# Output rows' norms: row sums inside VectorE's passes, squares on ScalarE, no wide GpSimd passes; the router's logits on four column strips of TensorE

## The chip, the cores and the metric

The kernel runs on one core of one Trainium2 chip. The metric is the device time of one execution in microseconds (us). A profile records one execution of the core: what each engine did and when (TensorE is PE, its weight loads PEld; VectorE is DVE, ScalarE is ACT, GpSimd is POOL, SyncE is SP), what it waited for, and the clock that TensorE was granted.

## The reference, cut to what matters

One layer of a streaming encoder on 1024 prompt rows and 64 sample rows of width 1024: a mixer, and then a mixture of 16 experts. The part that the change touches lies between the two, for every row:

```
mixed = w_out projection of the mixer's output
x   = LN_m(alpha * x + gate_m(c) * mixed)             # called x1 in the kernel; gains g, b
h   = LN0(x) * (1 + scale_f(c)) + shift_f(c)          # called h2
g_logits = h @ w_group + b_group                      # 4 columns
e_logits = h @ w_router + b_router                    # 16 columns
# group by argmax, two experts of the group by top_k, their weights by softmax
y   = sum over the two experts of weight * w_down(silu(h w_gate) * (h w_up))
x   = LN_f(alpha * x + gate_f(c) * y)
```

LN is a mean and a variance over the 1024 columns of a row, and LN0 is LN without gains.

## The kernel before, in words

Rows go in 9 tiles of up to 128, in the order `ORDER` = 0, 1, 2, 3, 8, 4, 5, 6, 7 (tile 8 has the 64 sample rows). Each engine has a program of its own, written in order; they meet at semaphores. Products of the projections and experts are split into three (high and low parts of both operands), so 48 matmuls of 512 columns make one tile's output projection.

The stage in question is a loop over those 9 tiles; n is a tile's place in `ORDER`, and `END` = 8 is the last place.

- TensorE (`out_part`, `h2_turned`, `logits`): for tile n the 48 matmuls of the projection into one of two pairs of banks; then `logits(n - 3)`, then `h2_turned(n - 2)`, eight transpositions of h2. After the last tile follow three rounds for the tiles still open, with `keep_clock` between them: matmuls of constants that fill the waits. `logits` multiplies the turned rows (weights of 128 columns) with `router_w` (20 columns moving), eight chunks, each as two instructions.
- VectorE: reads the projection (L1866), adds alpha x (L1868), takes mean and variance (`bn_stats`, L1616), subtracts the mean and applies the gain (L1881), makes the low part of tile n + 2's operand (`out_low`, L1791 and L1793), finishes x1 (L1888) and takes mean and variance of x1. The last tile is read in two halves (L1875 to L1877), and its h2 is made on VectorE too (L1897, L1900).
- GpSimd: the power -0.5 of each variance (`first_power` L2113, `norm_scalars` L639 to L641), and for the first eight tiles two passes of 1024 columns over h2, the scale (L2123) and the shift (L2125).
- ScalarE: the high part of tile n + 2's operand, the copy of the turned rows out of PSUM (L1500), and h2's normalisation (L1508).
- SP's queue: the loads of x, the stores of x1 and h2, and, behind the last of them, the weights of expert 0 (L773).

Behind the loop the router's decisions are made on VectorE (from L1905, which reads the logits), lists of rows are built, the first rows are gathered by a DMA, and a loop runs over 26 blocks of expert rows. The final norms, in the kernel's last stage, already use the two forms that the change takes up here: a pass on VectorE that also sums its result along the row (`accum_out`, L2032), and a `Square` on ScalarE with the negated mean as its bias, which sums the squares (L1585).

## Time and profile before

| what | before |
|---|---|
| median of 3 runs | 1382.14 us (1380.56 to 1382.39) |
| the profiled execution | 1381.44 us |
| its span, first to last instruction | 1379.6 us |
| TensorE busy over the span | 1307.4 us, 95% |
| VectorE, ScalarE, GpSimd busy | 768.3, 544.1, 318.0 us |

The profile is of an execution of its own; times in it count from the first instruction, and 1.84 us of the execution lie outside the span. Busy times of the whole span say little here: the stage of the change lasts from 675 to some 809 us, and it has limits of its own.

### The profile page before, as it was taken

To read this page: it belongs to the slowest core of one execution; us is meant where nothing else is said; L and a number is where in the kernel's file an instruction comes from. 1 tells how busy PE (TensorE), PEld (TensorE's weight loads), DVE (VectorE), ACT (ScalarE), POOL (GpSimd) and SP (SyncE) were. 2 spreads that over 40 slices of the span, in tenths; PEclk is the share of its full clock that TensorE was granted. 3 is DMA by queue.
4 is the path that set the end of the run, shared out by engine and by line. 5 is a ranking of instruction groups with operands and counts; after the bars stand their busy time and mean duration, and the time that the engine had idled before them with its cause. 6 is when DMAs were issued, how large, how long until landed. Compare 5 with 4: busy or idle time off the path is not lost.

```text
span 1379.6 us, 20025 instructions
## 1 busy us (share of the span) xinstructions
PE 1307.4 (95%) x7293; PEld 1015.5 (74%) x7294; DVE 768.3 (56%) x1040; ACT 544.1 (39%) x750; POOL 318.0 (23%) x449
## 2 busy tenths in 40 slices
PE   4899999999999989999999989999999999999984
PEld 2666678898787756666687877888888888888851
DVE  5734232424502066666699974557888242559648
ACT  0432012332212156556512242457776232357522
POOL 0123320002200066667256521000000000000053
PEclk9999999999999999999999999999999999999997
DMA  9853320102121171211432368867999261649764
GB/s 332 321 183 125 124 69 1 62 1 77 42 66 35 49 215 32 62 32 33 153 108 92 115 244 327 328 236 279 398 399 398 86 240 61 243 158 398 288 222 166
DMA packets 138776, 234.54 MB, mean 170 GB/s; under 512 B 57328, under 2 KB 58936, under 8 KB 138712
## 3 DMA queue, kind: packets, MB, share of 16 engines
q1 hardware_dynamic: 128440, 196.41, 40.3%
q0 software_dynamic: 6496, 23.60, 4.9%
q10 hardware_dynamic: 3776, 13.67, 2.4%
q8 instruction: 42, 0.69, 0.2%
q14 instruction: 22, 0.18, 0.0%
HBM read 197.96 MB, written 35.68 MB: 169 GB/s over the span
## 4 chain that ended last, share of the span: by engine, by line
PE 77%; POOL 7%; DVE 6%; issue 5%; DMA 2%; ACT 1%; SPq 1%; POOLq 0%; ACTq 0%; DVEq 0%
PE psum L834 71%; POOL arena L2101 5%; DMA arena<-in_w_ada_mix 2%; PE psum L1246 2%; PE psum L1061 1%; PE psum L1252 1%; DVE arena L2040 1%; DVE arena L2039 1%; PE psum L941 1%; DVE arena L2032 1%; DVE arena L2031 1%; PE psum L885 1%; PE psum L1155 0%; POOL arena L2098 0%; SPq L656 0%
## 5 line engine op out<-in xcount | busy, mean ns | idle before, releaser
L834 PE MATMUL psum<-arena 128*64 128x128 f32 (+8 forms) x1396 | 168.6, 374 | 25.5 <-DMA arena<-in_w_ada_mix 16.7
L834 PE MATMUL psum<-win_high,x_low 128*128 128x512 f32 (+1 forms) x432 | 168.7, 391 | 0.0
L834 PE MATMUL psum<-win_high,x_high 128*128 128x512 f32 (+1 forms) x416 | 166.3, 400 | 0.0
L834 PE MATMUL psum<-high,h_high 128*128 128x512 f32 x416 | 162.1, 390 | 2.5 <-DVE h_low L1986 2.5
L834 PE MATMUL psum<-win_low,x_high 128*128 128x512 f32 (+1 forms) x416 | 162.5, 391 | 0.0
L834 PE MATMUL psum<-high,h_low 128*128 128x512 f32 x416 | 162.2, 390 | 0.0
L834 PEld LDWEIGHTS psum<-arena 128*64 128x64 f32 (+4 forms) x1396 | 83.8, 144 | 103.5 <-issue 72.7
L1981 DVE TENSOR_TENSOR low_odd<-raw_odd,high 128x2048 fp32r<-128x2048 f32 x48 | 108.0, 2287 | 37.2 <-ACT high L1522 37.1
L1981 DVE TENSOR_TENSOR low_even<-raw_even,high 128x2048 fp32r<-128x2048 f32 x48 | 107.9, 2287 | 37.0 <-ACT high L1522 36.5
L1842 DVE TENSOR_TENSOR_SCAN arena<-arena,psum 128x512 f32<-128x512 f32 (+3 forms) x112 | 108.2, 1004 | 19.7 <-ACT arena L1477 19.5
L2101 POOL TENSOR_TENSOR arena<-arena 128x512 f32<-128x512 f32 (+4 forms) x116 | 96.8, 835 | 9.5 <-POOL arena L2095 0.3
L834 PEld LDWEIGHTS psum<-win_high,x_high 128*128 128x128 f32 (+1 forms) x416 | 75.6, 182 | 30.3 <-issue 8.7
L2158 POOL COPY smalls<-smalls 128x1 int32 x26 | 4.7, 181 | 404.4 <-PE psum L1246 398.9
L834 PEld LDWEIGHTS psum<-win_high,x_low 128*128 128x128 f32 (+1 forms) x432 | 78.6, 182 | 20.0
L1522 ACT ACTIVATE high<-raw_even 128x2048 fp32r<-128x2048 f32 x48 | 89.3, 1909 | 8.1 <-ACT arena L1563 5.3
L834 PEld LDWEIGHTS psum<-high,h_high 128*128 128x128 f32 x416 | 78.1, 188 | 18.9 <-issue 2.8
L1522 ACT ACTIVATE high<-raw_odd 128x2048 fp32r<-128x2048 f32 x48 | 89.3, 1912 | 6.4 <-ACT arena L1563 6.1
L834 PEld LDWEIGHTS psum<-high,h_low 128*128 128x128 f32 x416 | 78.1, 188 | 16.2
L834 PEld LDWEIGHTS psum<-win_low,x_high 128*128 128x128 f32 (+1 forms) x416 | 75.7, 182 | 17.3
L834 PE MATMUL psum<-high,a_high 128*128 128x512 f32 x208 | 83.3, 400 | 2.4
L834 PE MATMUL psum<-low_even,h_high 128*128 128x512 f32 x208 | 81.0, 390 | 0.0
L834 PE MATMUL psum<-low_odd,h_high 128*128 128x512 f32 x208 | 81.0, 389 | 0.0
(258 smaller groups left out, 2381.1 us busy)
## 6 DMA issues: line engine op xcount, KB each, us to landing
raw_even<-in_w_e_gate SPq DMA_DIRECT2D x8, 2048.0 KB, 10.9
raw_even<-in_w_e_up SPq DMA_DIRECT2D x8, 2048.0 KB, 16.8
raw_even<-in_w_e_down SPq DMA_DIRECT2D x8, 2048.0 KB, 15.6
raw_odd<-in_w_e_gate SPq DMA_DIRECT2D x8, 2048.0 KB, 10.6
raw_odd<-in_w_e_up SPq DMA_DIRECT2D x8, 2048.0 KB, 17.0
raw_odd<-in_w_e_down SPq DMA_DIRECT2D x8, 2048.0 KB, 16.0
win<-in_w_in SPq DMA_DIRECT2D x7, 2048.0 KB, 8.4
expert_rows<-arena ACTq DMA_DIRECT2D x26, 512.0 KB, 6.3
```

Source lines behind the costliest of these rows:

```text
L834: pe_last[0] = nc.tensor.matmul(*x, **y)
L885: last = nc.tensor.transpose(bank(H_BANKS[n % 4])[:, c0:c0 + r], xt[0:r, t, k * P:(k + 1) * P], ident[0:r, 0:r])
L941: last = nc.tensor.transpose(b[:, h * P:h * P + r], src[0:r, h, :], ident[0:r, 0:r])
L1061: last = nc.tensor.transpose(turned_weights(s)[0:r, a_, j * P:(j + 1) * P], weight[:, s % 3, a_, j * P:j * P + r], ident)
L1246: last = nc.tensor.transpose(psum[1][:, c // 4, (c % 4) * P:(c % 4 + 1) * P], hg[:, c * P:(c + 1) * P], ident)
L1252: last = nc.tensor.transpose(bank(at)[:, (f - f0) * P:(f - f0 + 1) * P], an[:, f * P:(f + 1) * P], ident)
L1522: A(chunk(high_w, c), chunk(raw_w[k], c), ACT.Copy).then_inc(s_wH, 1)
L1842: V.tensor_tensor_scan(out, out, floor, init, ALU.mult, ALU.max).then_inc(s_scan, 1)
L1981: TT(chunk(low_w[k], c), chunk(raw_w[k], c), chunk(high_w, c).bitcast(F32), ALU.subtract).then_inc(s_wL, 1)
L2031: done(TT(x, psum[2 * (t % 2)][0:r].rearrange("p a c -> p (a c)"), rows8[0:r, int(t == LAST)], ALU.mult), s_gated, t + 1)
L2032: done(STT(x, x1c[t][0:r], ALPHA, x, ALU.mult, ALU.add, accum_out=fin_nm[0:r, t:t + 1]), s_cacc, t + 1)
L2101: G.tensor_tensor(weight[:, s % 3, a_, 0:w], p[:, lo + 1:513], p[:, lo:512], ALU.subtract).then_inc(s_wm, 1)
```

## The change

Six things are changed, all in that stage.

1. VectorE's pass that adds alpha x also sums its result (`accum_out` into `ln_nmr`); a small operation makes the negated mean of it. The same is done for x1. `bn_stats` is gone for all tiles but the last.
2. ScalarE squares the rows less their mean and sums them (`accum_out` into `ln_ve`), twice a tile: once for x1's norm, once for h2's. It no longer normalises h2.
3. GpSimd keeps only operations of one column: scale and epsilon, and the power, twice a tile.
4. VectorE makes h2 of every tile in two passes; the second one (`h2_finished`) stands in the next tile's sequence.
5. The logits: `logit_parts(n)` keeps `router_w` (now padded to 32 columns) as the weights and moves the turned rows; chunk k goes to the strip of 32 PSUM partitions k % 4, two chunks added on each strip. ScalarE copies the 128 partitions out (`lparts`), and `logits(n)`, one matmul with a constant `pick`, adds the four strips and turns the result back. `logits` is one tile further behind than `logit_parts`.
6. The loads of the router's weights move in SP's queue from the projections' stage to behind the first two loads of x, since `router_w` now lies where the attention's queries were; the constant `pick` is loaded in their old place.

```diff
             def logits(n):
                 t = ORDER[n]
                 r = rows_of(t)
-                pe.wait_ge(s_hte, n + 1)
-                if n == 0:
-                    pe.wait_ge(s_router, 64)
-                for k in range(KC):
-                    last = mm(bank(6)[0:r, t * 20:t * 20 + 20], h2T[:, k, 0:r], router_w[:, k, :],
-                              start=(k == 0), stop=(k == KC - 1))
-                last.then_inc(s_lg, 1)
+                pe.wait_ge(s_hte, 2 * n + 2)
+                mm(bank(6)[0:r, t * 20:t * 20 + 20], lparts[:, 0:r], pick, start=True, stop=True).then_inc(s_lg, 1)
...
+            def logit_parts(n):
+
+                r = rows_of(ORDER[n])
+                pe.wait_ge(s_hte, 2 * n + 1)
+                if n == 0:
+                    pe.wait_ge(s_router, 80)
+                for k in range(KC):
+                    j = 32 * (k % 4)
+                    last = mm(bank(6)[j:j + 32, 256:256 + r], router_w[:, k, :], h2T[:, k, 0:r],
+                              start=(k < 4), stop=(k >= 4))
+                last.then_inc(s_lp, 1)
...
+                if n >= 4:
+                    logits(n - 4)
                 if n >= 3:
-                    logits(n - 3)
+                    logit_parts(n - 3)
                 if n >= 2:
                     h2_turned(n - 2)
...
+            def logit_parts(n):
+
+                r = rows_of(ORDER[n])
+                act.wait_ge(s_lp, n + 1)
+                A(lparts[:, 0:r], bank(6)[:, 256:256 + r], ACT.Copy).then_inc(s_hte, 1)
+
             for n in range(TILES + 2):
                 if n + 2 < TILES:
                     out_high("mixed", ORDER[n + 2])
+                if n < END:
...
+                    act.wait_ge(s_ve1, n + 1)
+                    A(xin[0:r, n % 2], t1[0:r, n % 2], ACT.Square, bias=ln_nmr[0:r, t:t + 1],
+                      accum_out=ln_ve[0:r, t:t + 1]).then_inc(s_sq5, 1)
                 v = n - 2
                 if v >= 0:
                     r = rows_of(ORDER[v])
                     act.wait_ge(s_ht, v + 1)
                     if v:
-                        act.wait_ge(s_lg, v)
+                        logit_parts(v - 1)
                     A(h2T[:, :, 0:r], psum[2].rearrange("p a (c q) -> p (a c) q", q=P)[:, :, 0:r], ACT.Copy).then_inc(s_hte, 1)
                 if n < END:
...
-                    act.wait_ge(s_nm2, n + 1)
...
-                    A(h2[0:r, n % 2], x1[0:r, n % 2], ACT.Identity, bias=ln_nmr[0:r, 9 + t:10 + t],
-                      scale=ln_rstd[0:r, 9 + t:10 + t]).then_inc(s_h2a, 1)
+                    act.wait_ge(s_ve2, n + 1)
+                    A(t1[0:r, n % 2], x1[0:r, n % 2], ACT.Square, bias=ln_nmr[0:r, 9 + t:10 + t],
+                      accum_out=ln_ve[0:r, 9 + t:10 + t]).then_inc(s_sq5, 1)
+            logit_parts(END)
...
+            def h2_finished(n):
...
+                dve.wait_ge(s_nm2, n + 1)
+                done(STT(h, h, ln_rstd[0:r, 9 + t:10 + t], rows5[0:r, 4 + int(t == LAST)], ALU.mult, ALU.add), s_h2, n + 1)
+
+            for n, t in enumerate(ORDER[:END]):
...
+                if n >= 2:
+                    dve.wait_ge(s_sq5, 2 * (n - 2) + 2)
+                dve.wait_ge(s_op, n + 1)
+                done(TT(x, psum[n % 2][0:r].rearrange("p a b -> p (a b)"), rows5[0:r, s], ALU.mult), s_ope, n + 1)
+                dve.wait_ge(s_x5[n % 2], 16 * (n // 2 + 1))
+                step(STT(x, xin[0:r, n % 2], ALPHA, x, ALU.mult, ALU.add, accum_out=ln_nmr[0:r, c]))
+                mean_negated(r, c, s_ve1, n + 1)
...
+                step(STT(y, x, ln_nmr[0:r, c], rows5[0:r, 6], ALU.add, ALU.mult))
+                if n >= 1:
+                    h2_finished(n - 1)
                 if n + 2 < TILES:
                     out_low("mixed", ORDER[n + 2])
                 dve.wait_ge(s_nm1, n + 1)
...
+                done(STT(y, y, ln_rstd[0:r, c], rows5[0:r, 7], ALU.mult, ALU.add, accum_out=ln_nmr[0:r, c2]), s_x1, n + 1)
+                mean_negated(r, c2, s_ve2, n + 1)
...
+                step(STT(h, y, ln_nmr[0:r, c2], rows5[0:r, 2 + s], ALU.add, ALU.mult))
+            h2_finished(END - 1)
...
             for n, t in enumerate(ORDER[:END]):
                 r = rows_of(t)
...
-                norm_scalars(step, G, r, 9 + t).then_inc(s_nm2, 1)
-                pool.wait_ge(s_h2a, n + 1)
-                step(G.tensor_tensor(h, h, rows5[0:r, 2 + s], ALU.mult))
-                first_power(n + 1)
-                G.tensor_tensor(h, h, rows5[0:r, 4 + s], ALU.add).then_inc(s_h2, 1)
...
+                for i, (col, ready) in enumerate(((t, s_nm1), (9 + t, s_nm2))):
+                    pool.wait_ge(s_sq5, 2 * n + i + 1)
+                    step(G.tensor_scalar(ln_ve[0:r, col:col + 1], ln_ve[0:r, col:col + 1], 1.0 / D, EPS, ALU.mult, ALU.add))
+                    power(col, r).then_inc(ready, 1)
...
             load_x(0)
             load_x(1)
+            sp.dma_start(router_w[:, :, 0:4], w_group[0].rearrange("(k p) n -> p k n", p=P)).then_inc(s_router, 16)
+            sp.dma_start(router_w[:, :, 4:20], w_router[0].rearrange("(k p) n -> p k n", p=P)).then_inc(s_router, 16)
```

The pieces stand in the order of the engines' programs: TensorE, ScalarE, VectorE, GpSimd, SP. In SP's loop the loads of x wait for ScalarE's first square of a tile instead of VectorE's variance. The last tile keeps its program on VectorE; its rows are now read by nothing on GpSimd but the two powers.

On VectorE, one tile in the middle of the loop (n = 6) stood so before (the numbers at L lines are those of each version's own text):

```order
L1866 TENSOR_TENSOR arena<-psum,arena 128x1024
L1868 SCALAR_TENSOR_TENSOR arena<-arena 128x1024
L1616 BN_STATS smalls<-arena 128x6 x2
L1617 BN_AGGR smalls<-smalls 128x2
L1856 TENSOR_SCALAR smalls<-smalls 128x1
L1881 SCALAR_TENSOR_TENSOR arena<-arena,smalls 128x1024
L1791 TENSOR_TENSOR x_low<-mixed,mix_high 128x4x128
L1793 TENSOR_TENSOR x_low<-hT,mix_high 128x4x128
L1888 SCALAR_TENSOR_TENSOR arena<-arena,smalls 128x1024
L1616 BN_STATS smalls<-arena 128x6 x2
L1617 BN_AGGR smalls<-smalls 128x2
L1856 TENSOR_SCALAR smalls<-smalls 128x1
```

And so stands the tile n = 7 and the step behind it in the changed kernel, the last tile of the new loop:

```order
L1906 TENSOR_TENSOR arena<-psum,arena 128x1024
L1908 SCALAR_TENSOR_TENSOR arena,smalls<-arena 128x1024
L1888 TENSOR_SCALAR smalls<-smalls 128x1
L1914 SCALAR_TENSOR_TENSOR arena<-arena,smalls 128x1024
L1896 SCALAR_TENSOR_TENSOR arena<-arena,smalls 128x1024
L1920 SCALAR_TENSOR_TENSOR arena,smalls<-arena,smalls 128x1024
L1888 TENSOR_SCALAR smalls<-smalls 128x1
L1927 SCALAR_TENSOR_TENSOR arena<-arena,smalls 128x1024
L1896 SCALAR_TENSOR_TENSOR arena<-arena,smalls 128x1024
L1937 TENSOR_TENSOR arena<-psum,arena 128x512
```

The two passes over the rows for mean and variance are gone, and two passes for h2 have come (L1927 and L1896); L1896 is `h2_finished`, first for the tile before, then, behind the loop, for this one, ahead of the last tile's first half (L1937).

On TensorE, the end of the stage stood so before, from the last projection's last matmul on (128x20 are the logits, L1155 the transpositions, 128x256 the fillers):

```order
L834 MATMUL psum<-x_high,x_low 128x512
L834 MATMUL psum<-smalls,arena 128x20 x8
L1155 MATMUL psum<-smalls,arena 128x128 x8
L834 MATMUL psum<-smalls 128x256 x2
L834 MATMUL psum<-smalls,arena 128x20 x8
L834 MATMUL psum<-smalls 128x256 x3
L1155 MATMUL psum<-smalls,arena 128x128 x8
L834 MATMUL psum<-smalls 128x256 x2
L834 MATMUL psum<-smalls,arena 128x20 x8
L834 MATMUL psum<-smalls 128x256 x6
L1155 MATMUL psum<-smalls,arena 128x128 x8
```

And so in the changed kernel:

```order
L841 MATMUL psum<-smalls 64x20
L841 MATMUL psum<-arena 32x128 x8
L1162 MATMUL psum<-smalls,arena 128x128 x8
L841 MATMUL psum<-smalls 128x256 x2
L841 MATMUL psum<-smalls 128x20
L841 MATMUL psum<-arena 32x128 x8
L841 MATMUL psum<-smalls 128x256 x3
L1162 MATMUL psum<-smalls,arena 128x128 x8
L841 MATMUL psum<-smalls 128x20
L841 MATMUL psum<-smalls 128x256 x2
L841 MATMUL psum<-arena 32x128 x8
L841 MATMUL psum<-smalls 128x256 x6
```

Each group of eight 128x20 products has become eight products of 32x128 and, one tile later, a single 128x20; the fillers are the same, with one more ahead of the very last single product.

## Rows read from the trace of the kernel before

**Rows 1.** Stage of the output rows: busy us of PE, PEld, DVE, ACT, POOL; clock.

```profile
675.00:788.00 113.00, 112.57 (x566) 91.79 (x567) 104.35 (x131) 27.43 (x41) 55.22 (x47) 1.00 0.36 123
```

**Rows 2.** Chain of waits that ended last, 640 to 860: start, us, what.

```profile
750.90 10.93 PE psum L834 x48
...
761.92 1.24 DVE arena L1866
...
837.90 11.17 PE psum L834 x48
```

**Rows 3.** Timeline of PE from the last tiles on: start, us, operation.

```profile
775.21 1.11 PE L834 MATMUL psum<-smalls,arena 128*64 128x20 f32 x16
...
788.10 1.85 PE L834 MATMUL psum<-smalls,arena 128*128 128x20 f32 x16
789.80 1.07 PE L1155 MATMUL psum<-smalls,arena 128*128 128x128 f32 x8
790.71 1.03 PE L834 MATMUL psum<-smalls 128*128 128x256 f32 x4
...
801.64 2.84 PE L834 MATMUL psum<-smalls 128*128 128x256 f32 x12
804.31 1.04 PE L1155 MATMUL psum<-smalls,arena 128*128 128x128 f32 x8
...
806.46 1.96 PE L834 MATMUL psum<-smalls,arena 128*128 128x20 f32 x16 [0.25 <-ACT arena L1500]
```

**Rows 4.** Timelines of PE and PEld: strips of 32 columns; products of 64x64.

```profile
22.23 1.92 PE L834 MATMUL psum<-arena 128*32 128x512 f32 x16 [1.68 <-DMA arena<-in_w_ada_mix]
...
692.42 0.19 PEld L834 LDWEIGHTS psum<-smalls 64*64 64x64 f32 x4 [0.35 <-issue]
```

**Rows 5.** Timeline of DVE, the last tile's steps.

```profile
787.75 0.69 DVE L1876 SCALAR_TENSOR_TENSOR arena<-arena 128x512 f32<-128x512 f32 x1
...
789.93 2.85 DVE L1876 SCALAR_TENSOR_TENSOR arena<-arena 128x512 f32<-128x512 f32 x1
...
795.41 3.24 DVE L1888 SCALAR_TENSOR_TENSOR arena<-arena,smalls 128x1024 f32<-128x1024 f32 x1
...
801.91 1.28 DVE L1900 SCALAR_TENSOR_TENSOR arena<-arena,smalls 128x1024 f32<-128x1024 f32 x1
...
808.53 0.33 DVE L1905 TENSOR_TENSOR smalls<-psum,smalls 128x160 f32<-128x160 f32 x1 [5.01 <-PE psum L834]
```

**Rows 6.** Timeline of POOL, the passes over h2 in the same stretch.

```profile
789.88 2.35 POOL L2123 TENSOR_TENSOR arena<-arena 128x1024 f32<-128x1024 f32 x1 [1.36 <-ACT arena L1508]
...
794.61 2.96 POOL L2125 TENSOR_TENSOR arena<-arena 128x1024 f32<-128x1024 f32 x1
```

**Rows 7.** Instructions of the final norms' lines: ns min/median/max, starts, forms.

```profile
L2032 DVE SCALAR_TENSOR_TENSOR arena<-arena x9: 1218/1226/1282, 1327.1 to 1367.2; 128x1024 f32<-128x1024 f32 x8, 64x1024 f32<-64x1024 f32 x1
L2032 DVE DVE_READ_ACCUMULATOR arena<-arena x9: 75/77/84, 1328.2 to 1368.3; 128x1 f32 x8, 64x1 f32 x1
L2033 DVE TENSOR_SCALAR smalls<-smalls x9: 146/154/155, 1328.3 to 1368.5; 128x1 f32<-128x1 f32 x8, 64x1 f32<-64x1 f32 x1
L1585 ACT ACTIVATE arena<-arena,smalls x9: 1147/1149/1150, 1328.5 to 1368.6; 128x1024 f32<-128x1024 f32 x8, 64x1024 f32<-64x1024 f32 x1
L1585 ACT ACTIVATION_READ_ACCUMULATOR arena<-arena,smalls x9: 186/187/188, 1329.6 to 1369.7; 128x1 f32 x8, 64x1 f32 x1
L2187 POOL TENSOR_TENSOR smalls<-smalls x9: 554/572/1417, 1332.7 to 1370.2; 128x1 f32<-128x1 f32 x8, 64x1 f32<-64x1 f32 x1
```

**Rows 8.** Instructions of ScalarE's line that copies 128 columns from PSUM.

```profile
L1554 ACT ACTIVATE a_high<-psum x78: 272/277/385, 850.1 to 1301.4; 128x128 fp32r<-128x128 f32 x52, 128x256 fp32r<-128x256 f32 x26
```

**Rows 9.** Timeline of SP's queue: when expert 0's second weights are issued.

```profile
813.00 0.38 SPq L773 DMA_DIRECT2D raw_even<-in_w_e_up  x1
```

**Rows 10.** Busy times by stretch, as in Rows 1, behind the router.

```profile
828.00:830.00 2.00, 2.00 (x6) 1.55 (x6) 2.00 (x2) 2.00 (x2) 2.00 (x1) 0.56 0.00 0
```

**Rows 11.** DMA issues: KB each, median us from issue to landing.

```profile
smalls<-in_w_router SPq DMA_DIRECT2D x1, 64.0 KB, 2.6
```

More of the change, by code:

```diff
@@ L243, in stream_step @@
         ret_d = tiny(36)
-        router_w = tiny(8, 20)
+        lparts = tiny(P)
+        pick = tiny(20)
         router_b = tiny(20)
@@ L1189, in _ @@
             keep_clock(2)
-            logits(END - 2)
+            logits(END - 3)
+            logit_parts(END - 2)
             for n, pause in ((END - 1, 3), (END, 6)):
@@ L1193, in _ @@
                 h2_turned(n)
+                logits(n - 1)
                 keep_clock(2)
-                logits(n)
+                logit_parts(n)
+            keep_clock(1)
+            logits(END)
             keep_clock(15)
@@ new lines, in _ @@
+                step(STT(h, y, ln_nmr[0:r, c2], rows5[0:r, 2 + s], ALU.add, ALU.mult))
+            h2_finished(END - 1)
+            n, t = END, ORDER[END]
+            x, x_in, h = t1[:, n % 2], xin[:, n % 2], h2[:, n % 2]
+            dve.wait_ge(s_sq5, 2 * (n - 2) + 2)
+            dve.wait_ge(s_x5[n % 2], 16 * (n // 2 + 1))
+            for hh in range(2):
+                cols = slice(hh * 512, hh * 512 + 512)
+                dve.wait_ge(s_op, n + 1 + hh)
+                step(TT(x[:, cols], psum[n % 2][:, hh], rows5[:, 0, cols], ALU.mult))
+                step(STT(x[:, cols], x_in[:, cols], ALPHA, x[:, cols], ALU.mult, ALU.add))
+                step(V.bn_stats(stats[:, hh, :], x[:, cols]))
@@ L1903, in _ @@
+            done(TS(ln_ve[:, 9 + t:10 + t], ln_mv[:, 9 + t, 1:2], EPS, None, ALU.add), s_ve2, n + 1)
+            dve.wait_ge(s_h2o[n % 2], 16 * (n // 2))
+            dve.wait_ge(s_ht, n - 1)
+            step(STT(h, x1[:, n % 2], ln_mv[:, 9 + t, 0:1], rows5[:, 2], ALU.subtract, ALU.mult))
+            h2_finished(n)
             step(V.memset(lg, 0.0))
```

114 lines of the change are left out of this document (48 added, 66 removed).

## The prediction

> **What bounds the kernel now.** First the busy times of the stage. From 675 to 788 us TensorE is busy for 112.6 of 113 us at full clock, VectorE for 104.4, ScalarE for 27.4, GpSimd for 55.2 [rows 1]. So TensorE sets the pace, VectorE follows with 8% to spare, and ScalarE has room. Second, the chain of waits, to see where that stops being true. It lies on TensorE, 48 matmuls of a tile's projection at 10.93 us, up to 761.8, and then changes to VectorE at 761.92, which is by then the later of the two. TensorE's first expert block begins at 837.90 [rows 2], and from there the chain is one block after another.
>
> Two lengths follow. Call E the moment at which the last projection's matmuls are issued and TensorE turns to what is left: 788.10, where the logits behind it start [rows 3]. Call D the moment at which VectorE reads the logits: 808.53 [rows 5]. D - E is 20.4 us. The kernel gets shorter by what E moves forward and by what D - E shrinks, if nothing behind D hangs on something else.
>
> Why is D - E so long? VectorE's steps for the last tile show it. The pass L1876 takes 0.69 us on the first half and 2.85 on the second; L1888 takes 3.24, while the pass of the same kind at 801.91 takes 1.28 [rows 5]. GpSimd's two passes over h2 of the tile before run from 789.88 for 2.35 us and from 794.61 for 2.96, right over these two [rows 6]. So on this one tile (2.85 - 0.69) + (3.24 - 1.28) = 2.16 + 1.96 = 4.1 us of the chain are VectorE slowed by GpSimd's wide passes. The same happens in every tile, but there TensorE hides it.
>
> **The change part by part.**
>
> *VectorE's tile.* New sequence: product 1.24 [rows 2], sum with alpha x 1.23 and its accumulator's read 0.08, small step 0.15 [rows 7], gain 1.28 (as the pass at 801.91), h2 of the tile before 1.28, the low parts 2 x 0.69 [rows 5], x1 with its sum 1.28 + 0.08, small step 0.15, h2's first pass 1.28. That is 9.4 us, with about 0.04 between steps 9.8. The statistics' passes are swapped for h2's, so busy time hardly falls; what falls away is the slowing.
>
> *Its two waits.* Each norm now goes VectorE, ScalarE, GpSimd, VectorE: the square 1.15 with its accumulator's read 0.19, one small step, taken as half the power's, and the power 0.57 [rows 7], with four hops some 2.5 us. Behind the first wait's start stand 1.28 + 1.28 + 1.38 = 3.9 us of VectorE's own work, behind the second 1.28 and the next tile's first 4 us. Both are covered, so I take nothing for them in the loop; uncovered they would be 5 us a tile. The power is 1.42 at the worst [rows 7], and 3.4 is still under 3.9. Two places have less cover: for n = 7 there is no low part, and `h2_finished(7)` comes right behind h2's first pass, so VectorE waits there about 1 us.
>
> *TensorE's logits.* Now a full tile's logits hold TensorE from 788.10 to 789.80, 1.70 us for 16 instructions; a tile of 64 rows about 1.0 [rows 3]. The single product is 2 such instructions, 0.21. The strips aren't in the trace in this size. The nearest row is a product on four strips of 32 columns with 512 columns moving: 1.92 us for the same 16 instructions [rows 4]; here 128 columns move, a quarter, 0.48. To that comes what it costs to change from full-width products to strips and back. The nearest row is a change to products of 64x64 in this very loop, where the weight loads stood still for 0.35 [rows 4]; but that is a gap in the loads, while the matmuls before it were still running. I take 0.17 for both changes, so 0.65 a tile; bounds 0.48 (changes free) and 0.48 + 2 x 0.35 = 1.18. If strips didn't run side by side it would be 1.7 or more, as now.
>
> The Trainium skill ("TensorEngine Tiling (Array Packing)", Instruction Overhead) gives each matmul some 60 cycles however few columns move; as an estimate that is 16 x 25 ns = 0.40 us here, under the 0.48 by the row, and the gain would be a little over a microsecond larger with free changes. The same page (Key Properties) says that a change of tiling mode drains TensorE, without a price; that is the rule against this part, and the second rival below is its mechanism.
>
> *E.* Ahead of E lie five logits: 4 x 1.70 + 1.0 = 7.8 us. In their place 4 x 0.65 + 0.55 for the strips and 4 x 0.21 for the single products: 4.0. TensorE needs 10.93 + 0.65 + 0.21 + 0.91 (transpositions, 789.80 to 790.71 [rows 3]) = 12.7 us a tile against VectorE's 9.8, so it keeps the pace. E comes 3.8 us earlier.
>
> *D - E.* VectorE first. It starts tile 7 when that projection ends, 12.6 us ahead of E; by the steps above it is through with `h2_finished(7)`, its wait included, 10.9 later, and with the last tile's first half after 13.1, so it takes the second half at E + 0.5. From there, h2 of the last tile took 14.0 us before (from the product some 0.73 ahead of 789.93 to 801.91 + 1.28 [rows 5]), less the 4.1 of slowing: 9.9. h2 is ready at E + 10.4.
>
> TensorE's own row of work up to there: single product, strips, transpositions 1.8; fillers are 12 instructions in 2.67 (801.64 to 804.31 [rows 3]), 0.22 each, so 0.9 for two; single product, and strips that wait for ScalarE's copies (0.27 for the strips' sums [rows 8], 1.03 for the turned rows: from the transpositions' end, 804.31 + 0.91, to the logits at 806.46, less two hops of 0.1) until 3.15, end 3.8; three fillers 5.15; transpositions 6.05; wait 0.35 for the strips' sums, single product, two fillers, strips, 8.15; six fillers, 10.8. So the fillers end just after h2 is there, and the last transpositions run from 10.8 to 11.7. Then come the two copies (13.15), strips with their pipeline's length (14.05), the copy of the sums (14.4), the last single product and the hop to VectorE: D at E + 15.0. The extra hop eats what the strips save here. D - E falls by 5.4, of which 4.1 is the slowing.
>
> *Behind D* the chain is 29.4 us of the router's small steps and the first gather, up to 837.90, and I leave it whole. The weights could be late: expert 0's second load is issued at 813.00, 4.5 us behind D [rows 9], since it waits for h2's store, which queues behind the first load. That load is issued right at E now, as its wait is over then, so the store no longer queues, and the second is issued near D. Nothing is late, and nothing gained: it is not on the chain.
>
> *The moved loads* land 2.6 us after issue [rows 11], four tiles ahead of their use. The load of `pick` and the memset of the padding are covered by the loop's slack on VectorE. Nothing.
>
> **Sum.** 3.8 + 5.4 = 9.2 us. Against the profiled execution, 1381.44, that gives 1372.2; this one ran 0.7 under the median, and I put the forecast between the two: 1372.4.
>
> **Rivals.**
>
> 1. *The sum as above.* With 0.48 to 0.85 for the strips and half a microsecond either way on VectorE's lag: 1370 to 1374.5. In this range lies also a dip of the clock: 828 to 830 us was granted 0.56, half rate (1.2 GHz), after TensorE had waited for the router's lists, and a filler took it [rows 10]. If the dip moves onto the first block, that costs about 1 us.
>
> 2. *The changes between strips and full width eat the saving.* At 1.18 a tile E moves by 3.8 - 5 x 0.53 = 1.1 only, and D - E holds four such groups, so it falls by 5.4 - 2.1 = 3.3: 4.4 in all, 1377. For it: the 0.35 in the loads [rows 4]. Against: TensorE itself shows no idle time there.
>
> 3. *Strips run one after another.* 1.75 each: E moves back by about 1, D - E falls by 1: no change, 1381. Against: 16 instructions of 512 columns in 1.92 us [rows 4] would take 7 one by one, at the filler's 0.22 for 256 columns.
>
> 4. *Slower: the round trip over three engines sets the loop's pace.* ScalarE works in order; its second square stands behind the copy of turned rows, which waits for TensorE. If the squares come late enough that both waits lie open, VectorE needs 9.8 + 5 = 14.8 a tile against TensorE's 12.7; over 8 tiles 17 us, less 9.2: 1389. It decides from 4.4 us of waiting a tile on. Against: the transpositions are done 1.8 us behind the projection, VectorE's second sum some 7 us behind it.
>
> **How the numbers follow.** First case 0.78, second 0.12, third 0.05, fourth 0.05. A difference under 0.2%, 2.8 us, can't be told from no change here. The first two are faster, the third is the same, and so is a fifth of the fourth, where only part of the waits lies open. Faster 0.90, same 0.06, slower 0.04. The range holds the first case with its sizes and the second: 1369 to 1377.
>
> **What would show it.** In the profile after: no pass on GpSimd over 1.5 us between 675 and 800; VectorE's passes of 1024 columns all at 1.2 to 1.3; VectorE waiting for TensorE once a tile, some 3 us; strips under 0.9 us a tile; E near 784.3 and D near 799.3; the first expert block near 828.7, with blocks behind it spaced as before. I am wrong if VectorE waits for GpSimd's power in the loop, if TensorE's tile stays over 13.2, or if the first block waits for weights.

## The result, and the profile after

The changed kernel takes 1367.11 us (median of 4 runs, 1364.82 to 1367.59), the kernel before 1381.35 beside it (4 runs, 1379.27 to 1382.39). The ratio is 0.9894, 95% interval 0.9878 to 0.9911: 14.2 us shorter. The forecast was 1372.4 and its range ended at 1369, so the direction was right and the size was not. The profiled execution took 1367.59 us, its span is 1365.0.

First TensorE at the stage's end in the timeline of the changed kernel (start, us, operation, in brackets the idle time ahead and what ended it); [rows 3] are the same place before.

```profile
744.18 0.29 PE L841 MATMUL psum<-smalls 128*128 128x20 f32 x2
...
756.84 0.29 PE L841 MATMUL psum<-smalls 128*128 128x20 f32 x2
...
781.82 0.29 PE L841 MATMUL psum<-smalls 128*64 128x20 f32 x2
782.04 0.65 PE L841 MATMUL psum<-arena 128*32 128x128 f32 x16
782.62 1.09 PE L1162 MATMUL psum<-smalls,arena 128*128 128x128 f32 x8
...
792.92 1.04 PE L1162 MATMUL psum<-smalls,arena 128*128 128x128 f32 x8
794.33 1.35 PE L841 MATMUL psum<-smalls 128*128 128x20 f32 x6 [0.37 <-ACT smalls L1516]
795.61 0.64 PE L841 MATMUL psum<-arena 128*32 128x128 f32 x16
```

E is 781.82. The single product holds TensorE for 0.22 us (781.82 to 782.04), the strips for 0.58 (to 782.62), and a full tile now takes 756.84 - 744.18 = 12.7 us, as forecast. VectorE in the same stretch, which answers to [rows 5]:

```profile
757.13 1.23 DVE L1906 TENSOR_TENSOR arena<-psum,arena 128x1024 f32<-128x1024 f32 x1 [3.30 <-PE psum L841]
...
775.40 1.28 DVE L1920 SCALAR_TENSOR_TENSOR arena<-arena,smalls 128x1024 f32<-128x1024 f32 x1 [0.50 <-POOL smalls L2163]
...
779.17 1.28 DVE L1896 SCALAR_TENSOR_TENSOR arena<-arena,smalls 128x1024 f32<-128x1024 f32 x1 [0.96 <-POOL smalls L2163]
...
783.40 0.69 DVE L1938 SCALAR_TENSOR_TENSOR arena<-arena 128x512 f32<-128x512 f32 x1
...
786.73 1.28 DVE L1946 SCALAR_TENSOR_TENSOR arena<-arena,smalls 128x1024 f32<-128x1024 f32 x1
...
797.16 0.32 DVE L1957 TENSOR_TENSOR smalls<-psum,smalls 128x160 f32<-128x160 f32 x1 [4.28 <-PE psum L841]
```

VectorE waits for TensorE once a tile, 3.3 us here (1.6 to 3.4 over the loop), and in the loop's last turn (n = 7) 0.50 and 0.96 us for GpSimd's power; in the turns ahead of it that power costs no wait. The two passes that took 2.85 and 3.24 us on the last tile [rows 5] take 0.69 and 1.28. D is 797.16, and D - E 15.3. The chain of waits behind it (start, us, what):

```profile
826.51 11.18 PE psum L841 x48
...
1297.30 2.64 DMA expert_rows<-arena
1302.09 5.19 DMA arena<-expert_rows,smalls
1307.41 12.28 PE psum L841 x32
```

The first expert block begins 29.35 us behind D, as before. It comes 11.4 us earlier than in [rows 2], but 2.1 of these are there before the stage's loop begins (its first projection starts at 673.36, before at 675.43), so the stage gave 9.3. The prediction's sum was 9.2. The other 5 of the 14.2 lie outside the stage, and the experiments are about them.

### The profile page after: what moved, and what is told of

It is laid out like the page before. It is cut to its first block, busy times and chain, and to the rows that moved or that the text cites. A ratio compares the mean times of both kernels' runs of the same rounds, so it can differ in the third digit from the quotient of the medians.

```text
span 1365.0 us, 20069 instructions
## 1 busy us (share of the span) xinstructions
PE 1297.5 (95%) x7313; PEld 1006.2 (74%) x7314; DVE 741.6 (54%) x1025; ACT 556.0 (41%) x783; POOL 275.6 (20%) x433
## 4 chain that ended last, share of the span: by engine, by line
PE 79%; POOL 7%; issue 5%; DVE 5%; DMA 2%; SPq 1%; ACT 1%; POOLq 0%; ACTq 0%; DVEq 0%
PE psum L841 73%; POOL arena L2153 5%; DMA arena<-in_w_ada_mix 2%; PE psum L1266 2%; PE psum L1068 1%; PE psum L1272 1%; DVE arena L2092 1%; DVE arena L2091 1%; PE psum L948 1%; DVE arena L2084 1%; PE psum L1162 1%; DVE arena L2083 1%; PE psum L892 1%; POOL arena L2150 0%; DMA arena<-expert_rows,smalls 0%
## 5 line engine op out<-in xcount | busy, mean ns | idle before, releaser
L841 PE MATMUL psum<-arena 128*64 128x128 f32 (+10 forms) x1540 | 169.8, 358 | 23.0 <-DMA arena<-in_w_ada_mix 14.7
L841 PE MATMUL psum<-smalls 128*128 128x256 f32 (+8 forms) x504 | 81.9, 322 | 1.0 <-ACT smalls L1516 0.7
## 6 DMA issues: line engine op xcount, KB each, us to landing
raw_even<-in_w_e_gate SPq DMA_DIRECT2D x8, 2048.0 KB, 11.4
```

Source lines behind the costliest of these rows:

```text
L841: pe_last[0] = nc.tensor.matmul(*x, **y)
```

## Experiments

Kernels of one group ran on one chip, beside runs of the kernel before.

### Both kernels again, and each half of the change alone

> The changed kernel once more, as it is, to see whether the 5 us that lie outside the stage come back. Theory 1 (they belong to one execution: where TensorE's clock dips is chance): the times move to 9.2 us under before, and the new profile has the row loop's last chain of 48 matmuls starting as late as before (675.4, not 673.4) or the final stage's first eight products at 6.3 us instead of 3.7. Theory 2 (they come with the changed program): 13 to 15 us under before again, the loop's chain again near 673.4 and the final stage's first products again 3.7 us. In both the stage itself, from the loop's last chain to the first expert block, is 9.3 us shorter than before.

> The kernel before once more, for a second profile of it. Theory 1: its fourth product of the first stage (3.45 us, at half clock) and the first products of its final stage (6.33 us, at half clock) are fast this time in one place or the other, and the time follows by 1.5 to 3.7 us. Theory 2: both are slow again, and the time agrees with the other runs of before within 1 us.

The third kernel has the new norms with the old logits:

```diff
-    mm(bank(6)[0:r, t * 20:t * 20 + 20], lparts[:, 0:r], pick, start=True, stop=True).then_inc(s_lg, 1)
+    for k in range(KC):
+        last = mm(bank(6)[0:r, t * 20:t * 20 + 20], h2T[:, k, 0:r], router_w[:, k, 0:20],
+                  start=(k == 0), stop=(k == KC - 1))
```

> The new norms with the old logits (eight products of 128x20 a tile, turned rows as the weights). By the steps of the prediction the moment E doesn't move (five logits of 1.70 and 1.0 us stay ahead of it) and D - E falls by 4.1 to 4.7, the slowing of VectorE: 4.1 to 4.7 us under before. If the 5 us outside the stage come with the norms or with the moved loads, which are in here too, 9 to 10 under before; if they come with the new logits, or with nothing in particular, 4 to 5.

The fourth is the kernel before with `logit_parts`, `logits`, the copy of the sums and the moved loads of the changed one; in TensorE's loop:

```diff
-                if n >= 3:
-                    logits(n - 3)
+                if n >= 4:
+                    logits(n - 4)
+                if n >= 3:
+                    logit_parts(n - 3)
```

> The old norms (GpSimd's wide passes stay) with the new logits on four strips. By the steps of the prediction E moves by up to 4.2 us, if VectorE, busy 104.4 of 113 us with the passes slowed by GpSimd, can follow TensorE's 12.7 us a tile; if it can't, by 2 to 3; D - E stays at 20.4 plus some tenths for the additional hop. So 2 to 4 us under before. With the 5 us outside the stage, if they come with the moved loads or the logits: 7 to 9 under before.

| kernel | median us (runs) | ratio to before, 95% |
|---|---|---|
| changed, again | 1368.61 (6) | 0.9883 [0.9857, 0.9909] |
| before, again | 1381.99 (12) | 0.9996 [0.9976, 1.0016] |
| norms only | 1377.59 (9) | 0.9955 [0.9932, 0.9977] |
| strips only | 1378.19 (12) | 0.9968 [0.9950, 0.9986] |

The two repeats enter the stage's loop at the same moment, 673.49 (changed) and 673.51 (before). So the 2.1 us ahead of the stage were chance of one execution: theory 1 holds for these. Over the twenty profiles of this document the loop begins between 671.67 and 676.92 us, without an order by kernel. For the whole excess it fell, since the times stay 13.4 us apart. In these two profiles E is 781.95 and 786.20, D 797.29 and 806.62, the first block 825.90 and 835.29: the stage gives 9.4 us again. Then the chain of waits of the kernel before, repeated, where the rows after the stage differ:

```profile
835.29 12.79 PE psum L834 x48
...
1307.51 4.15 DMA expert_rows<-arena
1313.82 5.49 DMA arena<-expert_rows,smalls
1319.45 14.59 PE psum L834 x32
```

Its first block takes 12.79 us instead of 11.2, the store of the last expert rows lands in 4.15 instead of 2.64, and the final products take 14.59 instead of 12.28. TensorE's timeline at the final products, first in the repeat of before, then in that of the changed kernel; and two stretches of the repeat of before by busy time, whose third number from the end is the granted clock:

```profile
1319.45 5.98 PE L834 MATMUL psum<-arena 128*128 128x512 f32 x8 [4.62 <-DMA arena<-expert_rows,smalls]
```

```profile
1306.65 6.65 PE L841 MATMUL psum<-arena 128*128 128x512 f32 x8 [2.88 <-DMA arena<-expert_rows,smalls]
```

```profile
835.00:839.00 4.00, 3.71 (x10) 2.95 (x11) 4.00 (x3) 0.00 (x0) 0.07 (x1) 0.62 1.04 398
1319.00:1325.00 6.00, 5.55 (x8) 2.52 (x9) 0.00 (x0) 0.00 (x0) 2.65 (x3) 0.57 0.97 362
```

Behind these waits TensorE runs at the lower level, 1.2 GHz, for some us (0.62 and 0.57 granted over the two stretches). The changed kernel does so too in its repeat, after 2.88 us of waiting; after 2.80 in its first profile it did not (3.67 us for the same eight).

The halves say something of their own. By the same marks from the loop's first product on, norms alone (VectorE's timeline at D) leave E where it was (112.67 us behind it, before 112.69) and take 2.5 us off D - E, not 4.1: VectorE is done early and then waits 7.32 us for TensorE, whose own row of old logits and fillers now sets the pace. Strips alone move E by the full 4.2 (108.46), but D - E is 25.7, 5.2 longer: VectorE is still slowed by GpSimd, ScalarE's copies of the strips' sums stand behind the old normalisation of h2, TensorE waits 2.35 us for such a copy and later 2.76 for GpSimd's pass, and the clock falls (TensorE's timeline in strips only, then a stretch of it by busy time, 0.53 granted).

```profile
804.51 0.32 DVE L1937 TENSOR_TENSOR smalls<-psum,smalls 128x160 f32<-128x160 f32 x1 [7.32 <-PE psum L841]
```

```profile
786.44 0.40 PE L842 MATMUL psum<-smalls 128*128 128x20 f32 x2 [2.35 <-ACT smalls L1516]
```

```profile
786.00:800.00 14.00, 9.92 (x55) 6.68 (x56) 13.30 (x14) 2.50 (x5) 8.20 (x8) 0.53 0.37 113
```

So in the stage, in one profile of each, the halves give 2.5 and lose 1.0, and together they give 9.4. Both medians fell as forecast (4.2 under before for 4.1 to 4.7; 3.6 for 2 to 4), but not by the forecast's steps: that is luck. Norms-only has a store of 3.72 us, and strips-only one of 2.63 with 3.67 us for its first eight final products: what makes the end longer goes with the old logits.

### The packet in the store

The DMA rows around the store say what is different. This is the repeat of before, 1304 to 1319 us (queue, packets, MB, share; then issues with KB and us to landing):

```profile
q8 instruction: 1, 0.02, 0.6%
...
expert_rows<-arena ACTq DMA_DIRECT2D x1, 512.0 KB, 4.1
```

The three profiles with old logits so far (the repeat, the first, norms only) have one packet of instructions there, the three with strips none. The changed kernel's TensorE program is ten matmul calls longer ahead of the expert loop (nine single products, one filler). So ten calls were added to the kernel before, and ten taken from the changed one, at equal fill time; of the two places one is shown of each:

```diff
 # before, ten more
-            keep_clock(15)
+            keep_clock(10)
+            keep_clock(10, w=128)
 # changed, ten fewer
-            keep_clock(15)
+            keep_clock(5)
+            keep_clock(5, w=512)
```

> The kernel before, with ten of the fillers behind the stage (256 columns) each cut into two of 128: TensorE is busy as long, but its program has ten matmul calls more ahead of the expert loop, which is by how many the changed kernel's is longer. Theory F (the packet of instructions that is fetched while the last expert rows are stored comes from where TensorE's program crosses into its next piece): the packet no longer falls into the store, the store lands in 2.6 us instead of 3.5 to 4.15, TensorE's wait ahead of the final products is 2.8 to 2.9 instead of 3.6 to 4.6, and the kernel is 1 to 1.7 us shorter, up to 4.4 where the first products then run at full clock (3.67 us, not 6). Theory G (the store is slower for another cause that comes with the old logits): 3.5 or more again, time as before.

> The changed kernel, with twenty of the same fillers replaced by ten of 512 columns: busy as long, but ten matmul calls fewer ahead of the expert loop. Theory F: the packet of instructions falls into the store again, the store lands in 3.5 to 4.2 us, TensorE waits 3.6 to 4.6 us ahead of the final products, and these begin at half clock (5.4 to 6.3 us): 1 to 4 us over the changed kernel, 1369 to 1372. Theory G: 2.6 us again, and the changed kernel's time.

Two more kernels of the group have longer fillers instead:

```diff
 # before
-            keep_clock(20)
+            keep_clock(28)
 # changed
-            keep_clock(20)
+            keep_clock(26)
 ...
             block_turn(0)
+            keep_clock(5)
```

> The kernel before with 28 fillers instead of 20 ahead of the final products, 8 x 0.44 = 3.5 us more, which covers TensorE's wait of 3.6 us there (and 3.5 of the 4.6 of the second profile). If the half clock in the first eight products is what costs 2.3 to 2.7 us, it is gone, the products take 3.7 us, and the kernel is 2.3 to 2.7 shorter. If the clock falls for another cause, nothing changes.

> The changed kernel with 26 fillers instead of 20 ahead of the final products (2.6 us more, in a wait of 2.8), and five more between the first block's transpositions and its products (2.2 us, in a wait of 2.54). By the reading of the dips: the first products of the final stage take 3.7 us in every execution and the first block is never at half clock, so the time is that of the changed kernel's best executions, 1364 to 1366, and scatters less. If the dips come from elsewhere: 1367 to 1369 as the changed kernel.

The kernel before with ten more, TensorE's timeline, and then the DMA issues (no queue of instructions has a packet in that stretch):

```profile
1317.57 3.67 PE L834 MATMUL psum<-arena 128*128 128x512 f32 x8 [2.93 <-DMA arena<-expert_rows,smalls]
```

```profile
expert_rows<-arena ACTq DMA_DIRECT2D x1, 512.0 KB, 2.7
```

The changed kernel with ten fewer, the same two views:

```profile
1309.13 5.37 PE L841 MATMUL psum<-arena 128*128 128x512 f32 x8 [3.74 <-DMA arena<-expert_rows,smalls]
```

```profile
q8 instruction: 1, 0.02, 0.5%
...
expert_rows<-arena ACTq DMA_DIRECT2D x1, 512.0 KB, 3.6
```

Theory F's packet moves in both directions: with ten calls it leaves the store or comes back, the landing follows (2.66 and 3.58 us), and so does the wait (2.93 and 3.74). The other profiles agree: five of the twenty have a packet of instructions between the store's issue and its landing, and there it takes 3.51 to 4.15 us; in the other fifteen it takes 2.63 to 2.67. The changed kernel with ten fewer takes 1370.28 us (ratio 0.9920 [0.9890, 0.9949]), 1.7 over its repeat and 3.2 over its first timing. But the kernel before with ten more takes 1382.11 (0.9999 [0.9977, 1.0020]): the forecast gain of 1 to 1.7 us isn't there in the median, although its profiled execution took 1377.0. Its twelve times fall into two groups, four at 1374.5 to 1377.4 and eight at 1380.6 to 1385.5.

Fillers ahead of the final products (28) bring these to full clock also where the packet is in the store:

```profile
1320.65 3.67 PE L834 MATMUL psum<-arena 128*128 128x512 f32 x8 [0.91 <-DMA arena<-expert_rows,smalls]
```

1379.34 us, ratio 0.9977 [0.9955, 0.9999]: shorter, but the profiled execution (1380.70) lost 1.4 us at its first block (12.57 us instead of 11.17), so the forecast 2.3 to 2.7 isn't cleanly there. The changed kernel with fillers at both places takes 1366.63 (5 runs, 1365.32 to 1372.49): 0.5 to 2 us less than without, which these runs can't tell from nothing. The forecast of 1364 to 1366 with less scatter was missed.

### Ten tiny calls, GpSimd's passes, one strip, a covered version

```diff
 # before, ten tiny calls
             keep_clock(17)
+            keep_clock(10, w=2)
```

> The kernel before, with its fillers left as they are, and ten matmul calls of 2 columns more behind the last fillers ahead of the lists, where TensorE waits 1.25 us for VectorE. Theory F, as with the ten more calls made by cutting fillers: no packet of instructions in the store, which lands in 2.6 to 2.7 us; TensorE waits 2.8 to 2.9 us; 1 to 1.7 us shorter, up to 4.4 where the final products begin at full clock. Cutting fillers into halves left the median where it was, with times on both sides; if that came from the cut fillers and not from the packet, the median is 1377 to 1379.5 now. If the packet is worth no time, 1380 to 1382.

1382.40 us (1.0006 [0.9990, 1.0021]), profiled at 1375.66, the store in 2.66: the same two groups, five at 1375.7 to 1379.2 and seven at 1382.3 to 1384.4. The median lies nearest the forecast for a packet that is worth no time (1380 to 1382), and splitting the fillers is not the reason for the two groups.

```diff
 # changed, two passes on GpSimd
+            pool.wait_ge(s_op, TILES + 1)
+            step(G.tensor_tensor(zero_rows, rows5[:, 2], rows5[:, 4], ALU.mult))
             pool.wait_ge(s_ve1, TILES)
             power(ORDER[END], P).then_inc(s_nm1, 1)
+            step(G.tensor_tensor(zero_rows, rows5[:, 2], rows5[:, 4], ALU.add))
```

> The changed kernel with GpSimd's two wide passes put back for the last tile alone, over rows that nobody reads: one from E on, one behind its power. If such passes slow VectorE's, as the prediction's 4.1 us have it: the alpha pass on the second half takes 2.85 us, x1's pass 3.2, D comes 4.1 us later, and the kernel takes 1371 to 1373. If the slowing in the kernel before had another cause: both passes as in the changed kernel (0.69 and 1.28), and its time.

Timelines of GpSimd, VectorE and TensorE in this kernel:

```profile
781.61 2.36 POOL L2172 TENSOR_TENSOR arena<-arena 128x1024 f32<-128x1024 f32 x1 [2.90 <-PE psum L841]
...
786.33 3.00 POOL L2175 TENSOR_TENSOR arena<-arena 128x1024 f32<-128x1024 f32 x1
```

```profile
783.04 1.49 DVE L1938 SCALAR_TENSOR_TENSOR arena<-arena 128x512 f32<-128x512 f32 x1
...
787.15 3.25 DVE L1946 SCALAR_TENSOR_TENSOR arena<-arena,smalls 128x1024 f32<-128x1024 f32 x1
```

```profile
795.46 1.09 PE L1162 MATMUL psum<-smalls,arena 128*128 128x128 f32 x8 [2.74 <-DVE arena L1896]
796.92 2.50 PE L841 MATMUL psum<-smalls 128*128 128x20 f32 x6 [0.37 <-ACT smalls L1516]
```

GpSimd's passes end at 783.97 and 789.33, VectorE's 0.56 and 1.07 us later, about their own length (0.69 and 1.28): the slowing is a wait for GpSimd's whole pass. The Trainium skill ("SBUF — State Buffer", Terms) says that the two engines share a pair of ports that is held for a full instruction, and that the loser blocks; these rows agree. Not every pass waits: in the kernel before, the statistics of a tile (764.44, 1.42 us, as elsewhere) ran inside a GpSimd pass (764.02, 2.66 us). VectorE loses 0.80 + 1.97 = 2.8 us here, since the first pass overlaps less. The kernel takes 1374.53, 6 to 7.4 over the changed one, where 1371 to 1373 were forecast. D - E is 20.5, 5.2 more, of which these are 2.8: TensorE then waits 2.74 us for h2, and the six instructions behind it take 2.50 us instead of 1.35, at the lower clock (0.57 granted from 796 to 801 us).

```diff
 # changed, all chunks on one strip
-                    j = 32 * (k % 4)
+                    j = 0
...
-                              start=(k < 4), stop=(k >= 4))
+                              start=(k == 0), stop=(k == KC - 1))
```

> The changed kernel with all eight chunks of the logits on one strip of 32 partitions (the copy and the last product then take 32 rows). If the four strips run side by side: the 16 instructions, one after another, take 1.7 us and more instead of 0.58, TensorE's tile 13.8 instead of 12.7, E comes 5 us later and D - E grows by 1 to 2, so 1373 to 1376. If the strips give nothing, and 32 columns of weights alone make them cheap: 0.6 us and the changed kernel's time.

```profile
792.15 1.93 PE L841 MATMUL psum<-arena 128*32 128x128 f32 x16
794.02 1.09 PE L1162 MATMUL psum<-smalls,arena 128*128 128x128 f32 x8
```

The same 16 instructions hold TensorE for 1.87 us instead of 0.58: side by side the strips save 1.3 a tile. The kernel takes 1382.31 (1.0012 [0.9999, 1.0026]), where 1373 to 1376 were forecast: E - first product is 115.0 us instead of 108.5, and D - E 20.8 instead of 15.3, since the four groups of the end stand one behind the other on TensorE. These 12.0 us are most of the gain; its profiled execution, 1385.13, also began the loop late (676.92) and its final products at the lower clock (5.19 us for the first eight).

```diff
 # changed, covered
-            keep_clock(20)
+            keep_clock(26)
 ...
             block_turn(0)
+            keep_clock(5)
 ...
-            for n, pause in ((END - 1, 3), (END, 6)):
+            for n, pause in ((END - 1, 3), (END, 5)):
 ...
-                    act.wait_ge(s_ht, v + 1)
                     if v:
                         logit_parts(v - 1)
+                    act.wait_ge(s_ht, v + 1)
```

> The changed kernel with 26 fillers instead of 20 ahead of the final products, five between the first block's transpositions and its products, and two edits at the stage's end: ScalarE copies the strips' sums ahead of its wait for the turned rows, and five fillers instead of six stand ahead of the last transpositions, which h2 reached 0.3 us late. The last two take 0.5 to 0.6 us off D - E (14.8 instead of 15.34); with the fillers the final products take 3.7 us and the first block is at full clock: 1364.5 to 1366.5. If the dips elsewhere decide: 1367 to 1368.

1367.01 us (6 runs, 1364.79 to 1367.78; 0.9899 [0.9880, 0.9917]). D - E is 14.55, 0.8 less, so the two edits at the stage's end do what they should; over the whole they can't be told from the changed kernel, and the forecast of 1364.5 to 1366.5 was missed.

### Where the upper group of times comes from

> A second profile of the kernel before with the ten tiny matmul calls. If it falls into the fast bunch: 1374 to 1379, as the first. If into the slow one (1380.6 to 1385): the loss shows as a stretch at half clock, either at the first block (1.4 to 1.6 us lost) and the final products (2.3 to 3.0), which together make 4 to 4.6, or at another place. The store lands in 2.6 to 2.7 us in either bunch, by theory F; with the packet back in it 3.5 or more.

> A third profile of the same kernel, with the same expectations: 1374 to 1379 with no further stretch at half clock, or 1380.6 to 1385 with one; the store in 2.6 to 2.7 us in both.

Both profiled executions fell into the upper group, 1384.19 and 1382.31 us, with the store at 2.66. TensorE's timeline of the first, then the same stretch by busy time:

```profile
796.16 1.09 PE L1155 MATMUL psum<-smalls,arena 128*128 128x128 f32 x8 [2.28 <-POOL arena L2126]
797.09 1.61 PE L834 MATMUL psum<-smalls 128*128 128x256 f32 x4
798.49 3.48 PE L834 MATMUL psum<-smalls,arena 128*128 128x20 f32 x16
801.80 5.47 PE L834 MATMUL psum<-smalls 128*128 128x256 f32 x12
```

```profile
797.00:807.00 10.00, 10.00 (x35) 8.37 (x34) 4.73 (x8) 1.02 (x1) 3.15 (x9) 0.52 1.00 320
```

At the stage's end of the kernel before TensorE waits 2.28 us for GpSimd's pass over h2. In these two executions the clock falls behind it (0.52 over these 10 us, 0.51 in the second), and D - E is 24.9 instead of 20.4. In both, the first block (12.8 us) and the final products (5.3 us for the first eight) run at the lower clock too. The changed kernel has no such wait: its longest there is 0.37. Eight fillers instead of three cover the wait:

```diff
-            for n, pause in ((END - 1, 3), (END, 6)):
+            for n, pause in ((END - 1, 8), (END, 6)):
```

The next kernel covers the other two waits instead, with 26 fillers ahead of the final products and five ahead of the first block's; the two behind it cover the stage's end, alone and with those.

> The same kernel with 26 fillers instead of 20 ahead of the final products and five between the first block's transpositions and its products, as in the changed kernel with fillers. If the slow bunch is made by half clock behind these two waits, it is gone: nearly all times at 1373 to 1377. If it is made elsewhere, the two bunches stay, at 1373 to 1376 and 1380 to 1385.

> The kernel before with the ten tiny calls, and with eight fillers instead of three ahead of the transpositions that wait 2.28 us for GpSimd's pass over h2 (5 x 0.44 = 2.2 us more, inside the wait). If that wait lets the clock fall: the slow bunch is gone, the median goes from 1382.4 to 1375 to 1379, TensorE's matmuls between E and D are all at full rate (0.22 us a filler instruction), D - E 20.4. If the fall at 797 has another cause: two bunches again, 1382 in the median.

> The same, and 26 fillers ahead of the final products and five ahead of the first block's products: the kernel before with the packet out of the store and its three waits covered. If the gain over the stage's 9.3 us is made of packet and clock: 1373 to 1377, which is 7.5 to 10.5 over the covered changed kernel of the same call. If the change has a further effect of its own: 12 to 14 over it.

> The covered changed kernel once more, on the chip of the two runs before it: 1365 to 1367.8 again; no time over 1369 if the waits that are left (up to 0.7 us at the stage's end, 0.4 ahead of the final products) are too short for the clock to fall.

| kernel before with ten tiny calls, and ... | median us | times | ratio to before, 95% |
|---|---|---|---|
| nothing more | 1382.40 | 1375.66 to 1384.38 | 1.0006 [0.9990, 1.0021] |
| the first block's and the final wait covered | 1378.66 | 1374.99 to 1380.97 | 0.9984 [0.9965, 1.0003] |
| the wait at the stage's end covered | 1378.35 | 1374.36 to 1382.69 | 0.9977 [0.9957, 0.9996] |
| all three covered | 1375.73 | 1375.50 to 1377.19 | 0.9948 [0.9931, 0.9965] |
| the covered changed kernel | 1366.63 | 1366.22 to 1369.18 | 0.9888 [0.9868, 0.9908] |

The last three rows are of one group (before beside them 1381.21), the first two of others (1380.20 and 1379.85), so rows of different groups are compared by their ratios.

With the stage's end covered the matmuls there run at full clock:

```profile
791.29 3.70 PE L834 MATMUL psum<-smalls 128*128 128x256 f32 x16
795.12 1.09 PE L1155 MATMUL psum<-smalls,arena 128*128 128x128 f32 x8
```

By the ratios each cover takes off 3 to 4 us, which is near the noise, and both together some 8, which is clear of it; the scatter goes with them. So the waits are the cause of this kernel's upper group, and not one of them alone: with the first two covered the times spread from 1375 to 1381, neither of the forecast's two cases, and with the stage's end covered three of twelve still lie at 1382.6 to 1382.7. Then before and changed kernel, both covered, stand 9.1 us apart. In their profiles the stage takes 10.1 us less, 0.8 of it by the covered version's own two edits; from D to the span's end they take 567.9 and 567.8 us. The final products of both, before and changed, run at full clock:

```profile
1316.19 3.67 PE L834 MATMUL psum<-arena 128*128 128x512 f32 x8 [0.30 <-DMA arena<-expert_rows,smalls]
```

```profile
1306.92 3.67 PE L841 MATMUL psum<-arena 128*128 128x512 f32 x8 [0.25 <-DMA arena<-expert_rows,smalls]
```

Two of the covered changed kernel's five times, 1369.16 and 1369.18, lie over the forecast's 1369, and no profile shows why.

## Why the prediction was wrong in size

**The stage was right in its sum.** From the loop's first product on, E came 4.2 us earlier (forecast 3.8) and D - E fell by 5.1 (forecast 5.4): 9.3 for 9.2, and 9.4 in the repeats. The strips take 0.58 us a tile (0.65, and more than the 0.40 of the estimate beside it), the single product 0.22 (0.21), VectorE waits some 3.3 us a tile (some 3) and 0.96 for the power of n = 7 (about 1), with 0.50 ahead of it that the prediction didn't have. Rivals 2 and 3 are out by the strips' rows. The one-strip kernel shows rival 3's time, "no change", though not its terms: E is 2.3 us later than before, not 1, and D - E 0.4 longer, not 1 shorter. Rival 4 is out: no wait for GpSimd in the loop until n = 7.

**Its split was not.** The prediction has 4.1 of D - E as passes of VectorE that GpSimd slows, all on the chain. The chain of the kernel before goes another way. Two of its pieces, and then TensorE's timeline at the second:

```profile
794.64 2.93 POOL arena L2125
797.62 1.11 PE psum L1155 x8
```

```profile
797.62 1.09 PE L1155 MATMUL psum<-smalls,arena 128*128 128x128 f32 x8 [2.29 <-POOL arena L2125]
```

Behind the first slowed pass it runs over GpSimd's own second pass, for which TensorE waits 2.29 us, and from there over TensorE's row. The second slowed pass, 3.24 us, isn't on it: VectorE's last pass ends at 803.19 [rows 5], 1.1 us ahead of the transpositions that use it [rows 3]. That GpSimd's passes slow VectorE's is shown by putting two back, but the norms alone take 2.5 us off D - E, about that wait, and the other 2.6 come with the strips, which shorten TensorE's own row. The sum held because the end of the changed kernel was laid out engine by engine (D at E + 15.0, measured 15.3); that the terms of the split add up to it is luck.

**The step that failed** is the condition under the sum, "if nothing behind D hangs on something else": all behind D was left whole, at a gain of nothing, and the sum was made against one profiled execution. Some 5 of the 14.2 us lie outside the stage. The prediction saw the clock as a cost that the change might bring ("about 1 us"), not as one that the kernel before pays. It pays it at the final products, 2.3 to 2.7 us in each of its two profiles, and at the first block, 1.6 us in one of them. At the stage's end its variants with ten more calls pay some 4.5 us behind the wait for GpSimd, in two of five profiles. The norms took this wait away; the logits, by ten matmul calls, moved a packet of instructions out of the last store, which shortened the last wait by 0.8 to 1.7 us. The final products of the kernel before and of the changed one, first profiles:

```profile
1319.36 6.33 PE L834 MATMUL psum<-arena 128*128 128x512 f32 x8 [3.56 <-DMA arena<-expert_rows,smalls]
```

```profile
1307.41 3.67 PE L841 MATMUL psum<-arena 128*128 128x512 f32 x8 [2.80 <-DMA arena<-expert_rows,smalls]
```

The two pairs of profiles come to their difference by different parts. In the first pair the spans are 14.6 us apart: 2.1 ahead of the loop by chance, 9.3 in the stage, 0.8 from the store's issue to the final products, 2.7 in their first eight matmuls, less 0.2 in the blocks. In the repeats it is 12.1: 9.4 in the stage, 1.6 in the first block, 1.7 from the store to the final products, less 0.7 since the changed kernel began these at the lower clock too. With the waits covered and the packet moved, the kernel before takes 1375.73, 5.5 under before in the same group; 9.3 and 5.5 are 14.8, for the 14.2 that were measured.

**Open.** How the 5.5 divide over many executions: the rows give the store and its wait 0.8 to 1.7, the rest being clock, which falls in some executions and not in others. That the upper times of the kernel before itself (1384 and more, 10 of 26 in the first group of runs) are falls at the stage's end is argued from its variants; both of its profiles show the wait and full clock behind it. Whether the ten calls, which stand behind that place, make the fall more frequent isn't shown either. The scatter also hides in the time what the packet alone is worth in the kernel before: with the ten calls its median doesn't move (1382.11 and 1382.40).

## What to carry to other kernels

Price a change by its stage, but list also each longer wait of TensorE (here 2.3 us and more) that it removes, shortens or makes, in the stage and far behind it: half clock after such a wait cost 1.4 to 4.5 us here, beside 9.3 saved in the stage. Where such waits lie, cover them by fillers in both versions before comparing them; the difference that is left (here 9 us of 14) is the change's own. Two halves of a change that load two engines need not add up: here they gave 2.5 and -1.0 in the stage alone, 9.4 together. And read what a pass costs off the chain: the slowed pass of 3.24 us here lay beside it.

## What the runs showed that was not expected

- One packet of instructions (0.02 MB) in the same stretch as a store of 512 KB made it land in 3.5 to 4.15 us instead of 2.63 to 2.67 (five profiles against fifteen); ten matmul calls some 500 us earlier in the program decide whether it falls there.
- Behind waits of 2.80 to 2.98 us ahead of the final products the clock fell in some executions (2.83, 2.88, 2.90, 2.92, 2.98) and not in others (2.80, 2.82, 2.93 twice, 2.97); behind 3.56 to 4.62 it fell in all four, behind 0.25 to 0.91 in none.
- On one strip the strips' 16 instructions take 1.87 us, on four 0.58, between products of full width.
